# Modulation tiles taken in pairs, weight loads moved ahead of them, cache copies issued by ScalarE, and the compressed-attention stage cut to its visible blocks

## The reference

```python
def ada_mod(c, w, b, n):
    m = jax.nn.silu(c) @ w + b
    return m.reshape(c.shape[0], n, 1, D_MODEL)
...
    s_c = jnp.einsum('bcgrd,bngd->bcgrn', qr, ctx['kc']).astype(jnp.float32) * scale
    m_c = (ctx['cend'][None, :] <= q_pos[:, None])[None, :, None, None, :]
    p_c = masked_softmax(s_c, m_c)
    o_c = jnp.einsum('bcgrn,bngd->bcgrd', p_c, ctx['vc'].astype(jnp.float32))
    imp = jnp.einsum('bcgrn,nj->bcgj', p_c, ctx['cmp_to_sel'])
...
    win_all = jnp.concatenate([state_nsa_win.astype(win.dtype), win], axis=1)
```

## Time and profile before

| | |
|---|---|
| median of 3 runs | 3684.43 us (3680.51 to 3685.9) |
| the profiled execution's own time | 3682.82 us |
| its span | 3681.0 us |
| PE busy | 3291.9 us, 89% |
| DVE busy | 1769.3 us, 48% |
| POOL busy | 1110.8 us, 30% |
| ACT busy | 942.5 us, 26% |
| mean granted TensorE clock | 0.941 of full speed |

### The profile page before, as it was taken

The page is one execution under the profiler, slowest core; times in us unless marked ns, Lnnn a source line. Parts: engine busy times, 40 slices in busy tenths (PEclk is TensorE's granted clock), DMA queues, the critical chain, the costliest instruction groups (busy, mean ns, idle before and its releaser), DMA issues. The chain is left out here.

```text
span 3681.0 us, 56062 instructions
## 1 busy us (share of the span) xinstructions
PE 3291.9 (89%) x22000; PEld 2951.9 (80%) x22000; DVE 1769.3 (48%) x3212; ACT 942.5 (26%) x1458; POOL 1110.8 (30%) x799
## 2 busy tenths in 40 slices
PE   6886979999999987979667999989687999999986
PEld 5885959999999985869545666657577999999985
DVE  4566046454454446340478888810217454454443
ACT  4544033121111114021124666600114111111111
POOL 1222203333333320323013555400121333333330
PEclk9997979999999997989789999989798999999998
DMA  4213432111111125320231000057202111111112
GB/s 180 73 58 102 145 138 68 46 47 47 46 47 47 46 89 191 119 81 29 99 120 54 2 2 2 2 171 238 98 26 84 47 46 47 47 47 46 47 51 90
DMA packets 75778, 272.75 MB, mean 74 GB/s; under 512 B 9306, under 2 KB 19938, under 8 KB 73330
## 3 DMA queue, kind: packets, MB, share of 16 engines
q1 hardware_dynamic: 73810, 262.99, 20.6%
q10 hardware_dynamic: 1728, 6.34, 0.4%
HBM read 245.47 MB, written 33.10 MB: 76 GB/s over the span
## 5 line engine op out<-in xcount | busy, mean ns | idle before, releaser
L1407 POOL TENSOR_TENSOR w_hi<-w_raw,misc 128x1024 fp32r<-128x1024 f32 x197 | 381.0, 1934 | 2050.5 <-DMA w_raw<-in_w 783.6
L1409 POOL TENSOR_TENSOR w_lo<-w_raw,w_hi 128x1024 fp32r<-128x1024 f32 x197 | 495.1, 2513 | 28.4 <-issue 0.4
L1612 PE MATMUL PA<-hB_hi,w_hi 128*128 128x344 f32 x1512 | 327.9, 326 | 47.4 <-DVE hB_lo L613 23.2
L1612 PE MATMUL PB<-hB_hi,w_hi 128*128 128x344 f32 x1488 | 319.1, 323 | 19.8 <-DVE hB_lo L1796 17.1
L1612 PE MATMUL PB<-hB_lo,w_hi 128*128 128x344 f32 x1488 | 317.6, 322 | 19.5 <-POOL w_lo L1409 19.5
L1612 PE MATMUL PA<-hB_lo,w_hi 128*128 128x344 f32 x1512 | 324.6, 323 | 0.0
L1612 PE MATMUL PA<-hB_hi,w_lo 128*128 128x344 f32 x1416 | 301.9, 322 | 0.0
L385 DVE SCALAR_TENSOR_TENSOR zb<-ub,vec,zb 128x1024 f32<-128x1024 f32 x48 | 158.3, 3297 | 297.1 <-ACT zb L357 297.1
L1612 PEld LDWEIGHTS PA<-hB_hi,w_hi 128*128 128x128 f32 x1512 | 257.2, 191 | 53.2 <-issue 23.9
L1612 PE MATMUL PB<-hB_hi,w_lo 128*128 128x344 f32 x1392 | 294.7, 320 | 0.0
L1612 PEld LDWEIGHTS PB<-hB_hi,w_hi 128*128 128x128 f32 x1488 | 251.9, 189 | 22.9 <-issue 18.3
(11 more groups left out here) (438 smaller groups left out, 6275.6 us busy)
## 6 DMA issues: line engine op xcount, KB each, us to landing
w_raw<-in_w SPq DMA_DIRECT2D x197, 512.0 KB, 3.3
pages<-in_pages SPq DMA_DIRECT2D x64, 384.0 KB, 4.2
cosT<-in_mw SPq DMA_DIRECT2D x32, 512.0 KB, 3.8
sinT<-in_mw SPq DMA_DIRECT2D x32, 512.0 KB, 4.5
mt<-in_mw SPq DMA_DIRECT2D x32, 512.0 KB, 3.9
x_dram<-X SPq DMA_DIRECT2D x3, 4128.0 KB, 12.0
X<-x_dram SPq DMA_DIRECT2D x3, 4128.0 KB, 13.7
mw<-in_mw SPq DMA_DIRECT2D x4, 2048.0 KB, 22.8
```

The source lines that it names most:

```text
L1407: pool.tensor_tensor(w_hi[b], w_raw[b], zero.broadcast_to([P, 1024]), ALU.add)
L1409: pool.tensor_tensor(w_lo[b], w_raw[b], w_hi[b].bitcast(F32), ALU.subtract).then_inc(sem("w_split"), 1)
L1612: mm = pe.matmul(PS[ps][:, c, 0:CH], w[:, w0:w0 + P], x[:, k, c * CH:(c + 1) * CH], start=(k == 0 and n == 0), stop=(k == K - 1 and n == 2))
```

## The change

Four things change.

1. Modulation tiles are taken in pairs p: one DMA of 1 MB into one buffer of two tiles, 16 matmuls of 256 columns instead of 32 of 128, one ACT copy of 256 columns, two folds. There is now one buffer for the loads and one for the copied rows, where there were two of each of half the size; the load of pair p waits until the rows of pair p-1 are done.
2. In the recurrent loop SP issues the weight loads one turn earlier, so ahead of the gate weights and modulation load of the turn before. The rows are computed before the fold of the pair before, both into PD, and only the first PD gate product waits for ACT's copy.
3. The five DRAM-to-DRAM copies are issued by ACT, directly behind `modulate(1, ...)` and ahead of its part of the first feed-forward layer.
4. In the compressed stage all operations work on the first 8i + 8 of the 64 block columns. The mask is added only at the edge (8 or 9 columns) and in PSUM, one tiny DVE operation per unit goes except in two units, and a tiny memset is added.

```diff
-    def rows_of(pe, e, landed, bank, cs=csil, tiles=mt):
-        pe.wait_ge(sem(f"mt_in{e}"), landed)
+    def rows_of(pe, landed, bank, cs=csil, tiles=mt):
+        pe.wait_ge(sem("mt_in"), landed)
         for k in range(KT):
             q = 32 * (k % 4)
-            mm = pe.matmul(bank[q:q + 32, 0:P], cs[:, NC * k:NC * k + 32], tiles[e][:, k * P:(k + 1) * P],
-                           start=(k < 4), stop=(k >= 4), skip_group_check=True)
+            mm = pe.matmul(bank[q:q + 32, 0:2 * P].rearrange("p (e n) -> p e n", n=P), cs[:, NC * k:NC * k + 32],
+                           tiles[:, :, k * P:(k + 1) * P], start=(k < 4), stop=(k >= 4), skip_group_check=True)
...
-    def row_out(act, d, bank, rows=mr):
-        act.wait_ge(sem("md_rows"), d + 1)
-        after(act, sem("md_fold"), d - 1)
-        act.activation(rows[d % 2], bank[:, 0:P], ACT.Copy).then_inc(sem("md_ev"), 1)
+    def row_out(act, p, bank, rows=mr):
+        act.wait_ge(sem("md_rows"), p + 1)
+        after(act, sem("md_fold"), p)
+        act.activation(rows, bank[:, 0:2 * P].rearrange("p (e n) -> p e n", n=P), ACT.Copy).then_inc(sem("md_ev"), 1)
...
+    def mod_load(sp, p, tiles=mt):
+        after(sp, sem("md_rows"), p)
+        t = p * 2 + FIRST
+        src = a["mw"][t:t + 2] if isinstance(p, int) else a["mw"][ds(t, 2)]
+        sp.dma_start(tiles, src.rearrange("t p n -> p t n")).then_inc(sem("mt_in"), 16)
...
         def shifted(u):
...
-            dve.tensor_tensor(s3, PA[:, u % 2, :].rearrange("p (h n) -> p h n", n=64), bc(C["cadd"][:, u % QT, :]),
-                              ALU.add).then_inc(sem("sc_read"), 1)
-            dve.drain()
-            dve.tensor_reduce(C["cm"], s3, AXX, ALU.max)
-            dve.drain()
-            dve.tensor_tensor(s3, s3, bn(C["cm"]), ALU.subtract).then_inc(sem("cs_ready"), 1)
-            dve.drain()
+            dve.tensor_tensor(ps[:, :, edge], ps[:, :, edge], bc(C["cadd"][:, i, edge]), ALU.add)
+            dve.drain()
+            dve.tensor_reduce(C["cm"], ps, AXX, ALU.max)
+            dve.drain()
+            dve.tensor_tensor(s3, ps, bn(C["cm"], i), ALU.subtract).then_inc(sem("cs_ready"), 1)
+            dve.drain()
+            dve.memset(dmark, 0.0).then_inc(sem("sc_read"), 1)
...
+        tile_load(2, 0)
+        tile_load(3, 1)
         with sp.Fori(1, KT) as j:
-            tile_load(j * 2, 0)
-            tile_load(j * 2 + 1, 1)
+            tile_load(j * 2 + 2, 0)
+            tile_load(j * 2 + 3, 1)
             gate_weights(j)
-            mod_load(sp, 0, j * 2, j * 2 - 1)
-            mod_load(sp, 1, j * 2 + 1, j * 2)
+            mod_load(sp, j)
...
         def lru_mod(j):
             after(pe, sem("gate_ev"), j * 3)
+            rows_of(pe, j * 16 + 16, PD)
             if not isinstance(j, int) or j > 0:
                 pe.wait_ge(sem("ev_act"), j * 2 + 2)
-                fold_of(pe, 0, j * 2 - 1, PB[:, 2, CH:CH + NC])
-                fold_of(pe, 1, j * 2, PB[:, 2, CH + NC:CH + 2 * NC])
-            rows_of(pe, 0, j * 16 + 16, PC)
-            rows_of(pe, 1, j * 16 + 16, PD)
+                fold_of(pe, j, PB[:, 2, CH:CH + 2 * NC])
...
         modulate(1, 2, HB, 4, 3)
+        for n in ("kwin", "vwin", "lst", "fst0", "fst1"):
+            act.dma_start(o[n], a[n]).then_inc(sem("out_copy"), 16)
         ffn_act(act, 0)
```

More of the change, by code:

```diff
@@ L184, in build @@
     pt = [awbuf(f"pt{i}", [P, 512]) for i in range(4)]
-    mt2 = [kvbuf(f"mt2_{i}", [P, NPR], F32, 33024 + 4096 * i) for i in range(2)]
-    mr2 = [kvbuf(f"mr2_{i}", [P, P], F32, 41216 + 512 * i) for i in range(2)]
+    mt2, mr2 = kvbuf("mt2", [P, 2, NPR], F32, 33024), kvbuf("mr2", [P, 2, P], F32, 41216)
     csil2, fold2 = kvbuf("csil2", [P, 96], F32, 42240), kvbuf("fold2", [P, NC], F32, 42624)
@@ L268, in rows_of, with fold_of @@
         mm.then_inc(sem("md_rows"), 1)
-    def fold_of(pe, e, evicted, out, rows=mr, f=fold):
+    def fold_of(pe, evicted, out, rows=mr, f=fold):
         pe.wait_ge(sem("md_ev"), evicted)
[L272 to L278, removed]
+        for e in range(2):
+            mm = pe.matmul(out[:, e * NC:(e + 1) * NC], rows[:, e, :], f, start=True, stop=True, skip_group_check=True)
+        mm.then_inc(sem("md_fold"), 1)
@@ L279, in mod_window @@
+    def mod_window(pe, p0, n, bank, out, added):
+        for p in range(p0, p0 + n):
+            pe.wait_ge(sem("md_ev"), p)
+            rows_of(pe, 16 * (p + 1), bank)
+            if p == p0:
                 after(pe, sem("md_add"), added)
             else:
-                fold_of(pe, (d - 1) % 2, d, out[:, (d - 1 - d0) * NC:(d - d0) * NC], rows, f)
-        d = d0 + n - 1
-        fold_of(pe, d % 2, d + 1, out[:, (n - 1) * NC:n * NC], rows, f)
-    def row_out(act, d, bank, rows=mr):
-        act.wait_ge(sem("md_rows"), d + 1)
-        after(act, sem("md_fold"), d - 1)
-        act.activation(rows[d % 2], bank[:, 0:P], ACT.Copy).then_inc(sem("md_ev"), 1)
@@ L702, in stage_c_pe @@
                 scores(u + 2)
[L703 to L710, removed]
+            pe.wait_ge(sem("md_ev"), 32 + u)
+            rows_of(pe, 16 * (33 + u), PA[:, 2, :], csil2, mt2)
+            if u >= 1:
+                if u % 4 == 1:
+                    pe.wait_ge(sem("md_add"), 13 + u // 4)
+                n = 2 * ((u - 1) % 4) * NC
+                fold_of(pe, 32 + u, PB[:, 2, n:n + 2 * NC], mr2, fold2)
             pe.wait_ge(sem("ct_ready"), u + 1)
@@ L732, in stage_c_act @@
                 exps(u + 1)
-            for d in (64 + 2 * u, 65 + 2 * u):
-                row_out(act, d, PA[:, 2, :], mr2)
+            row_out(act, 32 + u, PA[:, 2, :], mr2)
             act.wait_ge(sem("ctr_done"), u + 1)
@@ L765, in stage_c_dve @@
         dve.wait_ge(sem("att_in"), 16 * 5)
-        bc = lambda ap: ap.unsqueeze(1).broadcast_to([P, 8, 64])
-        bn = lambda ap: ap.unsqueeze(2).broadcast_to([P, 8, 64])
+        bc = lambda ap: ap.unsqueeze(1).broadcast_to([P, 8, ap.shape[1]])
+        bn = lambda ap, i: ap.unsqueeze(2).broadcast_to([P, 8, seen(i)])
+        dve.memset(C["im0"], 0.0)
         def shifted(u):
-            s3 = pbuf[u % 2][:, 0:512].rearrange("p (h n) -> p h n", n=64)
+            i = u % QT
+            ps, s3 = blocks(PA[:, u % 2, :], i), blocks(pbuf[u % 2][:, 0:512], i)
+            edge = slice(max(0, 8 * i - 1), seen(i))
             dve.wait_ge(sem("sc_done"), u + 1)
@@ L1338, in ffn_loads @@
             if l == 0:
-                mod_loads(sp, 40, 8)
+                for p in range(20, 24):
+                    mod_load(sp, p)
             sp.wait_ge(sem("x_ready"), x_done)
@@ L1358, in _ @@
         stream(T_KV, T_KV + 2)
-        mod_loads(sp, 54, 8)
+        for p in range(27, 31):
+            mod_load(sp, p)
         sp.wait_ge(sem("x_ready"), 16)
         sp.dma_start(x_dram, X.rearrange("p k t -> p (k t)")).then_inc(sem("x_spill"), 16)
-        mod_loads(sp, 62, 2)
-        sp.wait_ge(sem("md_fold"), 64)
+        mod_load(sp, 31)
+        sp.wait_ge(sem("md_fold"), 32)
         for dst, src in ((ident, a["ident"]), (perm, a["perm"]), (cosT, a["cos"]), (sinT, a["sin"])):
             sp.dma_start(dst, src).then_inc(sem("rope_in"), 16)
-        for n in ("kwin", "vwin", "lst", "fst0", "fst1"):
-            sp.dma_start(o[n], a[n]).then_inc(sem("out_copy"), 16)
         stream(T_KV + 2, T_Q)
@@ L1381, in _ @@
         sp.wait_ge(sem("csil_kept"), 1)
-        mod_loads(sp, 64, 32, mt2)
+        for p in range(32, 48):
+            mod_load(sp, p, mt2)
         smp_sp(sp)
@@ L1543, in _ @@
         lru_root(KT - 1)
-        for d in range(16, 24):
-            row_out(act, d, PC)
+        for p in range(8, 12):
+            row_out(act, p, PC)
         def evacuate(dst, psum0, ev0, n):
@@ L1883, in _ @@
         with dve.Fori(2, KT) as j:
-            add_bias(dve, j * 2 - 4, 2, pair)
+            add_bias(dve, j * 2 - 4, 2, pair, j - 1)
             lru_decay(j - 1)
```

137 lines of the change are left out of this document (68 added, 69 removed).

## The result

The changed kernel takes 3658.18 us (median of 4 runs, 3657.16 to 3662.12), the kernel before 3682.47 beside it: a ratio of 0.9935, with an interval of 0.9918 to 0.9952. The gain is 24.3 us. Its profiled execution took 3657.16 us, with a span of 3655.4 against 3681.0. I had forecast 3649 in 3624 to 3669.

The account below looks back on a forecast made before the run. PE, busy 89% of the span, was taken as the bound, so only its waits, lower clock or removed work pay. Terms -30.2 - 5 + 5 - 9.5 + 28 - 22 = -33.7 gave 3649 us; own range 3637 to 3664, widened by rivals to 3624 to 3669.

Parts of the forecast that it names:

- output projection to the first window: Pairs behind the output-projection tiles: PE's 0.39 us wait for ACT and some 0.2 us overhead go, 8 times: -5.
- Weight loads ahead: Recurrent loop: six late split waits go, with lower clock and part of ACT's second copy: -30.2, between -18 and -33.
- both circles: Loop turn: uc_ready at 9.0, needed at 9.9; tile B's add at 17.2 to 17.4, B starts at 17.5.
- Copies on ACT: Key/value split wait goes, -9.5; at the feed-forward start the third weight tile lands late behind the copies, +28.
- rivals 1 and 2: Feed-forward start: copies cheap, stall 0 to 5 us, 3621 to 3626 (0.17); or stall 14 + 2, 3637 (0.15).
- rival 2: Feed-forward start: all 8 packets of a load go between two large ones; stall 14 + 2, 3637 us; chance 0.15.
- Pairs in the windows: Modulation windows: one buffer must be emptied before loading, round 6.85 us; together +5, -4 to +11 by load time.
- behind the recurrent loop ACT is late anyway, 0: Window behind the recurrent loop: the single buffer's longer rounds cost nothing there, as ACT is late anyway: 0.
- rival 4: Slower: each us more of a pair's load costs 26 in all; gain gone at 6.1 us, 3706 at 7; chance 0.05.
- Compressed stage: Narrower DVE operations save 31 in all, but other circles lie close; 6.8 us a unit: -22, between 0 and -31.
- two other circles lie close: Compressed stage, per unit: pair's load and rows 6.0 to 6.9 us, PE's chain 5.4 to over 8; DVE 6.3.
- Rival 3: Compressed stage doesn't shorten, the single buffer or ACT's chain holding it at 8 us a unit: 3671; chance 0.12.

Follow-up runs that it names:

- the five other kernels with this stage: Changed kernel with, one at a time, copies on SP, small packets, old load order, copies spread, half loads; compressed stage untouched: stage 125.8 to 126.5 us.
- two buffers and ct first: Changed kernel with two buffers for the compressed stage's pair loads, and ACT copying ct ahead of the modulation rows: 3642.71 us, ratio 0.9894.

## Why the prediction was right

The total was right to 9 us, and its range held. Each term, by marks in both traces:

| term | forecast | measured |
|---|---|---|
| recurrent loop, from 54.7 us of the span to its last fold | -30.2 | 286.8 to 256.1: -30.7 |
| output projection to the first window | -5 | 127.7 to 121.5: -6.2 |
| windows | +5 | +2.2, +3.3, +4.6: +10.1 |
| start of the feed-forward layer (its first tile to the window behind it) | +28 | 853.9 to 878.7: +24.8 |
| key/value projection | -9.5 | 183.2 to 173.3: -9.9 |
| compressed stage | -22 | 138.8 to 122.5: -16.3 |

They make -28.2 of a span that fell by 25.6. Most of the rest is behind the rotation, in code that the change doesn't touch: 1717.4 us before, 1720.5 after, and 1717.2 to 1720.8 in the other kernels' profiles. That is the scatter of a profile. So no large misses cancelled: the windows and the compressed stage came out 10.8 us worse than forecast, and the layer's start 3.2 better, for the reason below. The upper end of the forecast's own range, 3664, was too low by its own terms: the worst of the loop and of the stage together make 22 us over 3649, 3671.

*Weight loads ahead* came out to half a us, with both circles where I had put them (the first tile of the changed kernel starts at 55.88, not 54.7, so the loop by itself is 31.9 us shorter), but the split between the parts was not mine: with pairs alone 10 us would have come, and the order adds 20.7. I had given the pairs and the order on PE only ACT's 2.4.

*Copies on ACT*: the mechanism was right. While the two copies ran in 64 KB packets, SP's queue got 5.6% of the engines' time against 89.7%, the weight tile was split from 36.6 us behind the first copy (I had said 34), and rivals 1 and 2 are out: a wait near 0 to 5, or of 14, would have shown. One step inside it was wrong. I had let two small packets go between two large ones, rival 2 all eight of a load; the trace has one, so about 7 and not 16 of an engine's 32 small packets had gone when its large ones ended. The rest then went in 8 us, faster than I had counted, and the two misses nearly cancel: that the landing came within 3 us is in part luck. So the rule of the Trainium skill (DMA: Bandwidth & Descriptors, Queues, rings and completion order), as I had read it, gave too short a wait: 14 us, measured 25.3. That the turns go by packets, as it says, agrees with the fall to 8.6 us at 4 KB.

The +24.8 is not the price of the copies alone. The view of PE's waits of the kernel before has a line for three waits in this layer, near 920, 1057 and 1194 us, for which the profile shows no releaser:

```profile
PE PA L1612 <- issue: 3.0, 3, 1.2
```

None of the twelve other kernels' profiles has them there, and no run shows why. Against the kernel with the copies on SP the layer's 878.7 us are 27.4 more, and that is what the forecast's 28 is to be held against.

*Pairs in the windows* was mis-sized: +10.1 for +5. A pair's load took 5.1 us, not 4.8, and a round 7.2, not 6.85. And the 0.6 us for ACT behind the last rows left out the fold that its copy waits for: from the end of those rows to the squares it was 1.3. With both, the squares of the first window came 24.05 us behind the rows, where I had summed up 22.2. And the step "behind the recurrent loop ACT is late anyway, 0" failed: four rounds outlast DVE's `s_lo` (ready at 326.9, the output projection starts at 337.5), which cost 2.2. They had before, too (357.6 and 366.1), so each us of a round counted there. The price of a load in rival 4 (3 us in each eight-tile window, 9 in all) had counted that place, the sum had not. The 4.4 us of the Trainium skill for the load (DMA: Bandwidth & Descriptors, Anatomy of one DMA), its fit for DMAs that GpSimd issues where SP issues these, was further off than the row.

*Compressed stage*: the term that failed in its parts. The unit, from the first to the last product with the values in 15 steps, came to 7.3 us (7.5 in the five other kernels with this stage), not 6.8 (before 8.1; full width with pairs 8.6), so that -16.3 is the kind end, and -12 to -13 what the five give. DVE's saving was right, 30.8 us for 31. Narrowing gave what I had said for the stage, about -21, but I had priced the pairs there at nothing, and they cost +8.4. I had seen the circles ("two other circles lie close") and taken a value between them in place of following what one buffer for the copied rows does: ACT's copy now waits for PE's fold, and `ct` for that copy, so PE stands 1.02 us where it stood 0.56, with the clock at 0.69 to 0.75 in place of 0.83. PE's waits for `ct` grew by 7.7 us, and at full width its busy time by 2.5 (91.1 to 93.6) with fewer instructions. What of this is the wait and what the clock that follows it stays open, since no run held the clock still.

Rival 3 is out by the stage's time, though what it named was at work: the single buffer and ACT's order held another 15.5 us. Rival 4 is out by its price: 5.1 us against the 6.1 from which it decides. What is left in a unit of 6.6 us with two buffers and ct first, 4.8 of them DVE's, was not followed. A second buffer for the copied rows was not tried.

## What to carry to other kernels

A large copy between DRAM and DRAM made PE wait nowhere once it was cut into small packets and pieces and issued where loads have slack; put ahead of the one load that has none, it cost its whole length (27.4 us of PE's time for copies that took 28). Taking away one wait in a stage with two circles of near length showed almost nothing until the other went as well, so a null result there is no proof that the wait didn't matter. One profile of a stage is a sample: the same stage took 122.5 us once and 125.8 to 126.5 five times. One large transfer into one buffer saves instructions and pays its round trip each time: count both.

## What was not expected of the hardware

The packet size of one queue's transfer set how long another queue's small load took, at the same bytes: 32.6 us to land beside 64 KB packets, 17.7 beside 4 KB ones. Beside the large packets the small ones went one for one (100 beside 96), so each waited for some 3 us of copy. Half a pair (512 KB) took 4.5 us to land and a pair 5.1, so half the bytes saved 0.6 us; two halves were under way at a time, and a whole tile of 512 KB had taken 3.8. And the same stage of the same code ran at a granted clock of 0.75 in one kernel and of 0.69 to 0.72 in five others: the same 545 matmuls, or one fewer, that the window counts were busy 88.5 us and 92.1 to 94.7.
